# Attention in a two-layer hybrid trunk: probabilities times values in 512-column products, scores of two key groups in alternate banks

## The chip, the cores and the metric

One core of one Trainium2 chip runs the whole program as a single launch. The metric is the device time of that launch in microseconds (us), lower is better; three runs of the kernel before are shown.

## The reference, cut to what matters

The program is two layers of a trunk over 256 tokens of 1024 channels. Each layer has a token mixer (a gated delta-rule branch and a sliding-window attention branch, fed by one input projection, merged by sigmoid gates) and then a channel mixer: dense SwiGLU in layer 0, eight experts in layer 1. The change touches only the attention branch:

```python
# 8 query heads of 64 channels in 2 key groups of 4; chunks of 64 tokens, a window of 2 chunks
s = einsum('bnqhgd,bnkhd->bhgnqk', qc, kb) * (dh ** -0.5)      # scores
m = maximum(max(s, axis=-1), sink)
p = exp(s - m)
denom = sum(p, axis=-1) + exp(sink - m)
p = p / denom
o = einsum('bhgnqk,bnkhd->bnqhgd', p, vb)                      # probabilities times values
```

## The kernel before, in words

Everything runs in float32 or in splits of it. Each weight matrix is streamed in units of 128x2048 through a ring of six buffers; ScalarE (ACT) rounds a unit to its high part `w_hi` (L759 in the mixers, L1046 in the experts), VectorE (DVE) subtracts to get the low part `w_lo` (L1799, L1963), and TensorE (PE) makes three products per tile from the parts (L1130 to L1132, L1124 to L1126). Every engine has its own program written out by hand, in order, and the engines meet through semaphores that only rise; there is no planner. A DMA refill of a ring buffer is issued by the SP queue once DVE has released the unit six places earlier.

The 256 tokens are two blocks `tb` of 128. The attention of one layer is a string of numbered tasks, and `ATT_BANK` says which of the eight PSUM banks each task writes. `scores(tb)` (L1328) makes the scores: block 0 has 128 keys, so four heads fill a bank of 512 columns and there are two banks (0 and 1); block 1 has 192 keys, two heads to a bank, four banks (2, 4, 5, 6). Each bank begins with one bf16 product that writes the mask (L1337, 128 rows of the array), then one float32 product per head (L1343) over the 64 channels of that head. The heads of key group 0 lie in rows 0 to 63 of `a_qT` and `a_kT`, those of group 1 in rows 64 to 127. Before, a bank holds heads of one group only, and the banks are made one after the other: for block 0 bank by bank group 0, then group 1; for block 1 two banks of group 0, then two of group 1. `am0` and `am1` are the masks, `G` = 2 groups, `J` = 4 heads in a group.

DVE takes the row maxima of each bank (L2040 in `row_max`), ACT takes the exponentials head by head (L918 in `exp_scores`), DVE divides (L2055), PE transposes (L1358, L1360 in `turn_p`), ACT copies the transposed probabilities to `a_pt` (L927), and `p_v(tb)` multiplies by the values `a_v`. In `p_v(0)` each head is one product of 128 columns over 128 keys (L1375). In `p_v(1)` each head takes two, one over the 64 keys in rows 64 to 127 (L1372) and one over 128 keys (L1373), which add up in the same 128 columns. All heads of a group use the same `a_v` as stationary operand. ACT and DVE then take the high and low part of the output (L934, L2062).

The order of the work on PE around it, per layer:

```python
                scores(0)
                scores(1)
                two_blocks(("qkvz", l, 7), 3)
                turn_p(0)
                pe.wait_ge(qkn_s, 2 * l + 1)
                pe.wait_ge(pe_s, TB * (l + 1))
                k_products(kT, 6)
                p_v(0)
                turn_p(1)
                pe.wait_ge(att_a, NATT_A * l + 6)
                one_block(("gate", l, 0), 0, 0)
                p_v(1)
```

after which come transposes (L1408), `k_products(qT, 4)` (L1386), the other half of gate 0 and the inversion of the delta rule in levels (from L1417). `warm` and `spread` (L1378) are products with 512 columns; `ada_piece` (L1143) makes products with a single column (L1145).

Of the kernel before, what the change touches and what calls it, by code (L numbers as in the profile page):

```python
# [16 lines left out]
P = 128  # L17
EPS = 1e-6
NEG = -1e30
CHUNK = 64  # L20
# [3 lines left out]
def build_program(nc, x, c, positions, ada_w, ada_b, norm_mix_w, norm_ffn_w, w_in, conv_w, a_log,  # L24
# [4 lines left out]
    T = x.shape[1]  # L29
# [4 lines left out]
    KEYS1 = 3 * CHUNK  # L34
    H = a_log.shape[1]
    DK = P
    NQH = sinks.shape[1]
    DH = CHUNK
    G = 2
    J = NQH // G  # L40
# [79 lines left out]
    for s, k in enumerate(split_keys):  # L120
        if k[0] in ("fg", "fu", "fd"):
# [3 lines left out]
            b, n_ffn = (2 - n_ffn) % NS_FFN, n_ffn + 1  # L125
        elif k == ("qkvz", 1, 0):
            b = 2
        elif k == ("mix", L - 1, 1, 1):
            b, last_in[2] = 2, split_keys.index(("wa", L - 1, 1))
        else:  # L130
            b = s % NS_MIX
# [45 lines left out]
    with ctx:  # L177
# [6 lines left out]
        ps = [ctx.enter_context(nc.psum_tensor(f"bank{b}", [P, 512], F32)) for b in range(8)]  # L184
# [21 lines left out]
        ident_b = sb("ident_b", [P, P], BF16)  # L206
# [55 lines left out]
        a_pt = wk(6144, 16, P)  # L262
        a_qk = wk(8192, TB, 10, DH)
        a_v = wk(10752, TB, P)
        a_qT = wk(9728, J, T)
        a_kT = wk(9472, T)
# [143 lines left out]
        att_ps = sem("attention_in_psum")  # L410
# [93 lines left out]
        ATT_BANK = (0, 1, 4, 0, 1, 2, 4, 5, 6, 0, 1, 4, 5, 0, 1, 2, 3, 2, 3)  # L504
        T_SCORE, T_TURN, T_PV = (3, 5), (9, 13), (11, 17)
# [237 lines left out]
        def _(act):  # L743
# [93 lines left out]
            for l in range(L):  # L837
# [74 lines left out]
                def exp_scores(tb):  # L912
                    keys, per = (P, KEYS1)[tb], (4, 2)[tb]
                    act.wait_ge(mx_s, TB * l + tb + 1)
                    act.activation(smax[:, tb, 3, :], smax[:, tb, 3, :], ACT.Exp)
                    for h in range(NQH):
                        n, m = divmod(h, per)
                        ins = act.activation(a_s[tb][:, h, :], ps[ATT_BANK[T_SCORE[tb] + n]][:, m * keys:(m + 1) * keys],  # L918
                                             ACT.Exp, bias=smax[:, tb, 0, h:h + 1], scale=float(DH) ** -0.5,
                                             accum_out=smax[:, tb, 2, h:h + 1])  # L920
                    ins.then_inc(pe_s, 1)
# [16 lines left out]
                for n in range(2):  # L938
                    b = att(n)
                    act.copy(a_qT[:, 2 * n:2 * n + 2, :].rearrange("p a b -> p (a b)"), b[:]).then_inc(att_a, 1)  # L940
                b = att(2)
# [112 lines left out]
            for n in range(4):  # L1054
                half, tb = divmod(n, TB)
# [65 lines left out]
        def _(pe):  # L1121
# [41 lines left out]
            def tokens(tb):  # L1163
                return slice(tb * P, (tb + 1) * P)
# [82 lines left out]
            for l in range(L):  # L1247
# [17 lines left out]
                else:  # L1265
                    pe.wait_ge(fold_s, 1)
                    for ko in range(KO):
                        ins = pe.matmul(ps[3][:, 0:E], ones[:], w_rs[:, ko, :], start=ko == 0, stop=ko == KO - 1)
# [19 lines left out]
                for kh in range(2):  # L1288
                    wh, wl = parts(("swq", l, kh), 4)
                    for tb in range(TB):  # L1290
                        for kk in range(4):
                            ko = 4 * kh + kk
                            ins = by_token(ps[2 + tb][:], hT_hi[:, ko, tokens(tb)], hT_lo[:, ko, tokens(tb)],
                                           wh[:, kk, :], wl[:, kk, :], ko == 0, ko == KO - 1)
# [6 lines left out]
                for tb in range(TB):  # L1301
                    for ko in range(KO):
                        ins = by_token(ps[tb][:, 0:2 * P + 2 * H], hT_hi[:, ko, tokens(tb)], hT_lo[:, ko, tokens(tb)],
                                       wh[:, ko, :], wl[:, ko, :], ko == 0, ko == KO - 1)
# [8 lines left out]
                for t in (0, 1):  # L1313
                    b = ps[ATT_BANK[t]]
                    for jj in range(2):
                        for tb in range(TB):
                            j = 2 * t + jj
                            ins = pe.transpose(b[:, jj * T + tb * P:jj * T + (tb + 1) * P],
                                               a_qk[:, tb, 2 * j:2 * j + 2, :].rearrange("p g d -> p (g d)"), ident[:])
                    ins.then_inc(att_ps, 1)  # L1320
                pe.wait_ge(ln_s, 4 * (l + 1))
                b = ps[ATT_BANK[2]]
                for tb in range(TB):
                    ins = pe.transpose(b[:, tb * P:(tb + 1) * P],
                                       a_qk[:, tb, NQH:NQH + G, :].rearrange("p g d -> p (g d)"), ident[:])
                ins.then_inc(att_ps, 1)

                def scores(tb):  # L1328
                    keys, per = (P, KEYS1)[tb], (4, 2)[tb]
                    am = (am0, am1)[tb]  # L1330
                    for n in range(NQH // per):
                        b = ps[ATT_BANK[T_SCORE[tb] + n]]
                        if tb and n == 0:
                            pe.wait_ge(qkv_s, 8 * l + 7)
                        if tb and n == 3:
                            pe.wait_ge(exps_s, 6 * l + 2)
                        pe.matmul(b[:, 0:per * keys], ident_b[:], am[:].unsqueeze(1).to_broadcast([P, per, keys]),  # L1337
                                  start=True, stop=False)
                        for m in range(per):
                            h = n * per + m  # L1340
                            g, j = divmod(h, J)
                            rows = slice(g * DH, (g + 1) * DH)
                            ins = pe.matmul(b[:, m * keys:(m + 1) * keys], a_qT[rows, j, tokens(tb)],  # L1343
                                            a_kT[rows, (T - KEYS1 if tb else 0):(T if tb else P)],
                                            start=False, stop=m == per - 1)
                        ins.then_inc(att_ps, 1)

                def turn_p(tb):
                    pe.wait_ge(pn_s, TB * l + tb + 1)
# [14 lines left out]
                def p_v(tb):  # L1364
                    pe.wait_ge(att_a, NATT_A * l + 5 + 4 * tb)
                    for g in range(G):
                        b = ps[ATT_BANK[T_PV[tb] + g]]
                        for j in range(J):
                            h = g * J + j
                            o = b[:, j * P:(j + 1) * P]  # L1370
                            if tb:
                                pe.matmul(o, a_v[CHUNK:P, 0, :], a_pt[CHUNK:P, h, :], start=True, stop=False)  # L1372
                                ins = pe.matmul(o, a_v[:, 1, :], a_pt[:, NQH + h, :], start=False, stop=True)  # L1373
                            else:
                                ins = pe.matmul(o, a_v[:, 0, :], a_pt[:, h, :], start=True, stop=True)  # L1375
                        ins.then_inc(att_ps, 1)

                def spread(lhsT, rows, banks):  # L1378
# [39 lines left out]
                for lev in range(1, LEVELS):  # L1418
                    for tb in range(TB):
                        if lev > 1:  # L1420
                            pe.wait_ge(xx_s, 12 * l + 2 * (lev - 2) + tb + 1)
                        for h in range(H):
                            n = tb * H + h
# [30 lines left out]
                    for tb in range(TB):  # L1454
# [3 lines left out]
                        for h in range(H):  # L1458
                            n = tb * H + h
# [307 lines left out]
        def _(dve):  # L1767
# [204 lines left out]
            for l in range(L):  # L1972
# [60 lines left out]
                def row_max(tb):  # L2033

                    keys, per = (P, KEYS1)[tb], (4, 2)[tb]
                    sm = smax[:, tb]
                    for n in range(NQH // per):
                        t = T_SCORE[tb] + n
                        dve.wait_ge(att_ps, NTASK * l + t + 1)
                        ins = dve.tensor_reduce(sm[:, 0, n * per:(n + 1) * per],  # L2040
                                                ps[ATT_BANK[t]][:, 0:per * keys].rearrange("p (h k) -> p h k", h=per),
                                                AX.X, ALU.max)
                    link(ins)
                    link(dve.scalar_tensor_tensor(sm[:, 1, :], sm[:, 0, :], float(DH) ** -0.5, sink_rows[:, l, :],
                                                  ALU.mult, ALU.max))
                    dve.tensor_tensor(sm[:, 3, :], sink_rows[:, l, :], sm[:, 1, :], ALU.subtract)
                    dve.tensor_scalar(sm[:, 0, :], sm[:, 1, :], -1.0, None, ALU.mult).then_inc(mx_s, 1)
# [438 lines left out]
```

## Time and profile before

| | |
|---|---|
| median of 3 runs | 1776.28 us (1775.56 to 1776.55) |
| span of the profiled execution, first to last instruction | 1772.6 us |
| device time of the profiled execution itself | not listed; against the median the span is 3.7 us shorter |
| TensorE busy | 98% |
| TensorE weight loads busy (beside the products) | 85% |
| VectorE busy | 83% |
| ScalarE busy | 61% |
| bytes read from HBM | 510.90 MB |

How to read it. A busy TensorE is one whose product records follow each other without a hole; a record's length includes the pipeline behind it, so the cost of one product is the distance between starts, not the length. A float32 product appears as two records with a weight load each; a product of the split parts (three per tile) as one. In the profile's chain of waits the work that ended last is followed back, each step to what released it. "Idle before" names the time an engine stood still in front of an instruction, and what ended it.

### The profile page before, as it was taken

To read this page: it belongs to the slowest core of one execution; us is meant where nothing else is said; L and a number is where in the kernel's file an instruction comes from. 1 tells how busy PE (TensorE), PEld (TensorE's weight loads), DVE (VectorE), ACT (ScalarE), POOL (GpSimd) and SP (SyncE) were. 2 spreads that over 40 slices of the span, in tenths; PEclk is the share of its full clock that TensorE was granted. 3 is DMA by queue.
4 is the path that set the end of the run, shared out by engine and by line. 5 is a ranking of instruction groups with operands and counts; after the bars stand their busy time and mean duration, and the time that the engine had idled before them with its cause. 6 is when DMAs were issued, how large, how long until landed. Compare 5 with 4: busy or idle time off the path is not lost.

```text
span 1772.6 us, 26724 instructions
## 1 busy us (share of the span) xinstructions
PE 1734.2 (98%) x10287; PEld 1510.4 (85%) x10290; DVE 1463.5 (83%) x1420; ACT 1085.5 (61%) x953; POOL 73.4 (4%) x131
## 2 busy tenths in 40 slices
PE   7999999999999999999999999999999999999997
PEld 6889999999998889987788888888888888888875
DVE  6978688878768665679988898988889889989898
ACT  4564355333345643567677777777777777777775
POOL 4010000000000100000000000010000000000000
PEclk9999999999999999999999999999999999999999
DMA  9735566988964332469999999999999999999994
GB/s 311 257 125 190 145 236 220 334 303 304 328 224 129 110 95 96 143 241 361 336 369 385 361 372 370 361 390 362 365 386 356 375 381 356 382 370 365 388 392 160
DMA packets 261447, 519.97 MB, mean 293 GB/s; under 512 B 12170, under 2 KB 75892, under 8 KB 261364
## 3 DMA queue, kind: packets, MB, share of 16 engines
q1 hardware_dynamic: 257988, 506.21, 80.4%
q0 software_dynamic: 3376, 12.58, 1.8%
q8 instruction: 60, 0.98, 0.2%
q14 instruction: 23, 0.19, 0.0%
HBM read 510.90 MB, written 7.86 MB: 293 GB/s over the span
## 4 chain that ended last, share of the span: by engine, by line
PE 87%; DVE 8%; ACT 2%; issue 2%; DMA 1%; POOL 0%; DVEq 0%; SPq 0%; ACTq 0%; POOLq 0%
PE bank L1124 17%; PE bank L1126 17%; PE bank L1125 17%; PE bank L1130 9%; PE bank L1131 8%; PE bank L1132 8%; DVE w_lo L1963 2%; DVE w_lo L1799 2%; PE bank L1726 1%; PE bank L1424 1%; PE bank L1461 1%; PE bank L1145 1%; DVE ada_acc L1817 1%; ACT w_hi L1046 1%; DMA ring<-in_ada_w_dram 1%
## 5 line engine op out<-in xcount | busy, mean ns | idle before, releaser
L1963 DVE TENSOR_TENSOR w_lo<-ring,w_hi 128x2048 fp32r<-128x2048 f32 x336 | 766.8, 2289 | 94.8 <-ACT w_hi L1046 90.1
L1046 ACT CAST w_hi<-ring 128x2048 fp32r<-128x2048 f32 x336 | 642.1, 1911 | 137.0 <-PE bank L1126 131.5
L1124 PE MATMUL bank<-w_hi,xg_hi 128*128 128x512 f32 x896 | 357.3, 399 | 0.7 <-DVE w_lo L1963 0.7
L1126 PE MATMUL bank<-w_hi,xg_lo 128*128 128x512 f32 x896 | 353.4, 394 | 0.0
L1125 PE MATMUL bank<-w_lo,xg_hi 128*128 128x512 f32 x896 | 352.9, 394 | 0.0
L1130 PE MATMUL bank<-hT_hi,w_hi 128*128 128x256 f32 x1040 | 300.6, 289 | 5.1 <-DVE w_lo L1799 4.3
L1131 PE MATMUL bank<-hT_lo,w_hi 128*128 128x256 f32 x1040 | 293.7, 282 | 0.0
L1132 PE MATMUL bank<-hT_hi,w_lo 128*128 128x256 f32 x1040 | 293.5, 282 | 0.0
L1799 DVE TENSOR_TENSOR w_lo<-ring,w_hi 128x2048 fp32r<-128x2048 f32 x94 | 214.5, 2289 | 63.3 <-ACT w_hi L759 63.1
L759 ACT CAST w_hi<-ring 128x2048 fp32r<-128x2048 f32 x94 | 179.0, 1907 | 58.3 <-PE bank L1132 57.8
L1130 PEld LDWEIGHTS bank<-hT_hi,w_hi 128*128 128x128 f32 x1040 | 198.4, 191 | 9.2 <-DVE w_lo L1799 4.0
L1124 PEld LDWEIGHTS bank<-w_hi,xg_hi 128*128 128x128 f32 x896 | 168.4, 188 | 42.1 <-issue 2.9
L1126 PEld LDWEIGHTS bank<-w_hi,xg_lo 128*128 128x128 f32 x896 | 168.3, 188 | 40.1
L1125 PEld LDWEIGHTS bank<-w_lo,xg_hi 128*128 128x128 f32 x896 | 168.5, 188 | 37.7
L1131 PEld LDWEIGHTS bank<-hT_lo,w_hi 128*128 128x128 f32 x1040 | 198.5, 191 | 1.9 <-issue 1.9
L1132 PEld LDWEIGHTS bank<-hT_hi,w_lo 128*128 128x128 f32 x1040 | 198.4, 191 | 0.0
L1124 PE MATMUL bank<-w_hi,h_hi 128*128 128x512 f32 x448 | 180.2, 402 | 0.0
L1125 PE MATMUL bank<-w_lo,h_hi 128*128 128x512 f32 x448 | 176.1, 393 | 0.0
L1126 PE MATMUL bank<-w_hi,h_lo 128*128 128x512 f32 x448 | 175.7, 392 | 0.0
L1817 DVE SCALAR_TENSOR_TENSOR ada_acc<-ring,c_silu,ada_acc 128x512 f32<-128x512 f32 x162 | 121.6, 751 | 6.0 <-DMA ring<-in_ada_w_dram 0.6
L1126 PEld LDWEIGHTS bank<-w_hi,h_lo 128*128 128x128 f32 x448 | 84.1, 188 | 19.3
L1124 PEld LDWEIGHTS bank<-w_hi,h_hi 128*128 128x128 f32 x448 | 84.2, 188 | 17.7 <-DVE w_lo L1963 0.2
(434 smaller groups left out, 2011.6 us busy)
## 6 DMA issues: line engine op xcount, KB each, us to landing
ring<-in_moe_w_gate_dram SPq DMA_DIRECT2D x112, 1024.0 KB, 7.4
ring<-in_moe_w_up_dram SPq DMA_DIRECT2D x112, 1024.0 KB, 7.3
ring<-in_moe_w_down_dram SPq DMA_DIRECT2D x112, 1024.0 KB, 7.2
ring<-in_ada_w_dram SPq DMA_DIRECT2D x48, 1024.0 KB, 6.4
ring<-in_w_in_dram SPq DMA_DIRECT2D x38, 1024.0 KB, 5.9
ring<-in_ffn_w_gate_dram SPq DMA_DIRECT2D x14, 1024.0 KB, 7.0
ring<-in_ffn_w_up_dram SPq DMA_DIRECT2D x14, 1024.0 KB, 6.8
ring<-in_ffn_w_down_dram SPq DMA_DIRECT2D x14, 1024.0 KB, 7.0
```

The costliest lines, as they stand in the source:

```text
L759: act.copy(w_hi[buf][:], ring[:, ring_slot, :]).then_inc(hi_ready, 1)
L1046: act.copy(w_hi[MOE_BUF[p % NS_MOE]][:], ring[:, p % RING, :]).then_inc(hi_ready, 1)
L1124: pe.matmul(o, xh, wh, start=start, stop=False)
L1125: pe.matmul(o, xh, wl, start=False, stop=False)
L1126: return pe.matmul(o, xl, wh, start=False, stop=stop)
L1130: pe.matmul(o, wh, xh, start=start, stop=False, skip_group_check=shared)
L1131: pe.matmul(o, wh, xl, start=False, stop=False, skip_group_check=shared)
L1132: return pe.matmul(o, wl, xh, start=False, stop=stop, skip_group_check=shared)
L1145: ins = pe.matmul(ps[bank][:, 4 * q + c:4 * q + c + 1], ada_acc[:, (NQ * l + q) % 2, c * P:(c + 1) * P], ones[:, 0:1], start=not begun, st ...
L1799: dve.tensor_tensor(w_lo[buf_of[s]][:], ring[:, u % RING, :], f32(w_hi[buf_of[s]][:]), ALU.subtract).then_inc(taken, 1)
L1817: ins = dve.scalar_tensor_tensor(acc, w[:, kk, :], ck, acc, ALU.mult, ALU.add)
L1963: dve.tensor_tensor(w_lo[b][:], ring[:, p % RING, :], f32(w_hi[b][:]), ALU.subtract).then_inc(taken, 1)
```

## The change

It does two things. `p_v` now makes one product of 512 columns for the four heads of a key group where it made four of 128 (in block 1 one over the 64 keys, one over the 128, per group). `scores` opens two banks at a time, one for each key group, writes both masks, and then issues the heads in turn: one of group 0 into the first bank, one of group 1 into the second, and so on. In block 1 the banks of a pair now hold heads (0, 1) and (4, 5), then (2, 3) and (6, 7), so `row_max` and `exp_scores` find the heads by a new formula, and the wait for `exps_s` stands before the third bank (task 7) where it stood before the fourth.

```diff
                     for h in range(NQH):
-                        n, m = divmod(h, per)
+                        g, j = divmod(h, J)
+                        n, m = G * (j // per) + g, j % per
...
-                    for n in range(NQH // per):
-                        b = ps[ATT_BANK[T_SCORE[tb] + n]]
-                        if tb and n == 0:
+                    for pair in range(NQH // per // G):
+                        banks = [ps[ATT_BANK[T_SCORE[tb] + G * pair + g]] for g in range(G)]
+                        if tb and pair == 0:
                             pe.wait_ge(qkv_s, 8 * l + 7)
-                        if tb and n == 3:
+                        if tb and pair == 1:
                             pe.wait_ge(exps_s, 6 * l + 2)
-                        pe.matmul(b[:, 0:per * keys], ident_b[:], am[:].unsqueeze(1).to_broadcast([P, per, keys]),
-                                  start=True, stop=False)
+                        for b in banks:
+                            pe.matmul(b[:, 0:per * keys], ident_b[:], am[:].unsqueeze(1).to_broadcast([P, per, keys]),
+                                      start=True, stop=False)
                         for m in range(per):
-                            h = n * per + m
-                            g, j = divmod(h, J)
-                            rows = slice(g * DH, (g + 1) * DH)
-                            ins = pe.matmul(b[:, m * keys:(m + 1) * keys], a_qT[rows, j, tokens(tb)],
-                                            a_kT[rows, (T - KEYS1 if tb else 0):(T if tb else P)],
-                                            start=False, stop=m == per - 1)
-                        ins.then_inc(att_ps, 1)
+                            for g, b in enumerate(banks):
+                                j = pair * per + m
+                                rows = slice(g * DH, (g + 1) * DH)
+                                ins = pe.matmul(b[:, m * keys:(m + 1) * keys], a_qT[rows, j, tokens(tb)],
+                                                a_kT[rows, (T - KEYS1 if tb else 0):(T if tb else P)],
+                                                start=False, stop=m == per - 1)
+                                if m == per - 1:
+                                    ins.then_inc(att_ps, 1)
...
                         b = ps[ATT_BANK[T_PV[tb] + g]]
-                        for j in range(J):
-                            h = g * J + j
-                            o = b[:, j * P:(j + 1) * P]
-                            if tb:
-                                pe.matmul(o, a_v[CHUNK:P, 0, :], a_pt[CHUNK:P, h, :], start=True, stop=False)
-                                ins = pe.matmul(o, a_v[:, 1, :], a_pt[:, NQH + h, :], start=False, stop=True)
-                            else:
-                                ins = pe.matmul(o, a_v[:, 0, :], a_pt[:, h, :], start=True, stop=True)
+
+                        def four(rows, at):
+                            return a_pt[rows, at + g * J:at + (g + 1) * J, :].rearrange("p a b -> p (a b)")
+
+                        if tb:
+                            pe.matmul(b[:], a_v[CHUNK:P, 0, :], four(slice(CHUNK, P), 0), start=True, stop=False)
+                            ins = pe.matmul(b[:], a_v[:, 1, :], four(slice(0, P), NQH), start=False, stop=True)
+                        else:
+                            ins = pe.matmul(b[:], a_v[:, 0, :], four(slice(0, P), 0), start=True, stop=True)
                         ins.then_inc(att_ps, 1)
...
-                        ins = dve.tensor_reduce(sm[:, 0, n * per:(n + 1) * per],
+                        at = J * (n % G) + per * (n // G)
+                        ins = dve.tensor_reduce(sm[:, 0, at:at + per],
```

## Rows read from the trace of the kernel before

**Rows 1.** The page: the span, and TensorE's busy time.
```profile
span 1772.6 us, 26724 instructions
...
PE 1734.2 (98%) x10287; PEld 1510.4 (85%) x10290; DVE 1463.5 (83%) x1420; ACT 1085.5 (61%) x953; POOL 73.4 (4%) x131
```

**Rows 2.** The page: the chain that ended last, by engine.
```profile
PE 87%; DVE 8%; ACT 2%; issue 2%; DMA 1%; POOL 0%; DVEq 0%; SPq 0%; ACTq 0%; POOLq 0%
```

**Rows 3.** Windows: stretch, then busy us and instructions by engine, clock, DMA share, GB/s.
```profile
104.00:111.26 7.26, 7.26 (x40) 4.89 (x38) 4.41 (x9) 5.88 (x20) 0.00 (x0) 1.00 0.03 8
601.79:609.05 7.26, 7.26 (x40) 4.89 (x38) 4.41 (x9) 5.88 (x20) 0.00 (x0) 1.00 0.03 8
...
126.68:133.25 6.57, 6.57 (x33) 4.76 (x33) 3.60 (x4) 0.58 (x1) 0.00 (x0) 1.00 0.21 75
624.47:631.05 6.58, 6.58 (x34) 4.76 (x34) 3.60 (x4) 0.58 (x1) 0.00 (x0) 1.00 0.20 72
...
800.00:1760.00 960.00, 953.89 (x4265) 771.98 (x4264) 863.07 (x648) 693.88 (x460) 38.38 (x31) 1.00 1.00 365
```

**Rows 4.** Timeline of PE through the scores, layer 0: start us, us, instruction.
```profile
104.00 0.38 PE L1337 MATMUL bank<-am,ident_b 128*128 128x512 bf16 x1
104.31 1.16 PE L1343 MATMUL bank<-work 64*128 64x128 f32 x8
105.40 0.39 PE L1337 MATMUL bank<-am,ident_b 128*128 128x512 bf16 x1
...
106.81 0.34 PE L1337 MATMUL bank<-am,ident_b 128*128 128x384 bf16 x1
107.07 0.92 PE L1343 MATMUL bank<-work 64*128 64x192 f32 x4
107.92 0.34 PE L1337 MATMUL bank<-am,ident_b 128*128 128x384 bf16 x1
```

**Rows 5.** Chain of waits, layer 0: what one record costs on PE, by kind.
```profile
104.17 0.22 PE bank L1337
...
134.29 1.79 PE bank L1386 x16
...
138.95 0.79 PE bank L1145 x8
...
141.63 3.44 PE bank L1380 x8
```

**Rows 6.** Timeline of PE in p_v(1), layer 0, to the transposes behind it.
```profile
126.68 0.48 PE L1372 MATMUL bank<-work 64*128 64x128 f32 x2
127.10 0.49 PE L1373 MATMUL bank<-work 128*128 128x128 f32 x2
127.52 0.48 PE L1372 MATMUL bank<-work 64*128 64x128 f32 x2
...
133.25 1.04 PE L1408 MATMUL bank<-ident,work 128*128 128x128 f32 x8
```

**Rows 7.** Timeline of PE: the first product of gate 0, layer 0.
```profile
123.64 0.36 PE L1130 MATMUL bank<-hT_hi,w_hi 128*128 128x256 f32 x1 [0.18 <-DVE w_lo L1799]
```

**Rows 8.** Timeline of DVE from the row maxima to gate 0's low part, layer 0.
```profile
109.13 1.68 DVE L2040 TENSOR_REDUCE smax<-bank 128x2 f32<-128x384 f32 x3
111.37 0.56 DVE L2040 TENSOR_REDUCE smax<-bank 128x2 f32<-128x384 f32 x1 [0.56 <-PE bank L1343]
...
118.22 1.22 DVE L2087 TENSOR_TENSOR work<-work,incl_blk 128x1024 f32<-128x1024 f32 x1
121.20 2.29 DVE L1799 TENSOR_TENSOR w_lo<-ring,w_hi 128x2048 fp32r<-128x2048 f32 x1 [1.76 <-ACT w_hi L759]
```

**Rows 9.** Timeline of ACT: exponentials that `exps_s` counts, and copies behind `turn_p(0)`, layer 0.
```profile
104.21 1.08 ACT L909 ACTIVATE work<-bank 128x512 f32<-128x512 f32 x2 [0.87 <-PE bank L1380]
...
117.75 1.07 ACT L927 COPY work<-bank 128x512 f32<-128x512 f32 x2 [1.87 <-PE bank L1360]
```

**Rows 10.** Who waited for whom: total us, times, longest us.
```profile
ACT ob_hi L934 <- PE bank L1373: 16.9, 4, 5.7
```

## Prediction

> **What bounds the kernel now.** I read the page first: TensorE is busy 98% of a span of 1772.6 us [rows 1], and the chain that ended last lies on it for 87% [rows 2]. Even the long expert stage, where the transfers are in flight all the time, has PE busy for 953.89 of 960 us [rows 3]. So what counts is time on PE, if nothing else becomes late. Next I cut windows around the parts that change. The scores take 7.26 us in either layer, `p_v(1)` takes 6.57 and 6.58 us, PE without a hole in all four, granted clock 1.00 (the level of 2.4 GHz), and hardly any transfer [rows 3]. The two layers are alike to 0.01 us, so I cost layer 0 and double it. Last come the timelines, for the distances between starts, and the chain of waits, for who is late behind.
>
> **The price list of one record.** A float32 product is two records. With 128 columns sixteen of them take 1.79 us: 0.112 each. With 512 columns eight take 3.44 us: 0.43 each. With a single column eight take 0.79 us: 0.099 each; streaming is nothing there, so this is the floor of a weight load and its issue [rows 5]. Four records of 128 columns (0.448) against one of 512 (0.43) is thus almost no gain: merging columns alone pays nearly nothing.
>
> **p_v(1): where the gain of the first part is.** From a 64-row product to the 128-row one behind it is 0.42 us, and 0.42 again to the next 64-row one [rows 6], although two records of 128 columns need 0.224. Each change between a 64-row and a 128-row product therefore costs 0.19 us. The 16 products with 15 changes among them and one of 0.10 at the end make 16 x 0.224 + 15 x 0.19 + 0.10 = 6.5, the window's 6.57. After, there are 4 products of two records with 512 columns, 3 changes, and the exit: 4 x 0.86 + 3 x 0.19 + 0.10 = 4.11. **Saved 2.46 us a layer**; if a change of rows were dearer behind a 512-column product by as much again, 1.9. All of it stands on PE, directly on the chain.
>
> **p_v(0).** Eight products become two: 16 x 0.112 = 1.79 to 4 x 0.43 = 1.72, so 0.07. I cost it at nothing, because gate 0 behind it waits for its low part anyway: PE stands 0.18 us in front of it [rows 7]. That weight chain starts at the transposes of `turn_p(0)` and runs through ACT and DVE, not through `p_v`. Without this cover it would be 0.14 us for both layers.
>
> **Scores, step by step.** A bank of block 0 is 1.40 us start to start, one of block 1 is 1.11 [rows 4]. A mask of 512 columns streams in 0.22 [rows 5], but the first 64-row product starts 0.31 to 0.32 behind it: 0.10 to get in. Eight records of 128 columns are 0.896, and the next mask comes 1.09 after them: 0.19 to get out. In block 1 the mask is 0.16 and 0.10, the four records of 192 columns take 0.85, of which 0.19 is the way out, so 0.165 each. With pairs of banks half of the ways in and out vanish. If the records just follow each other as now, block 0 is 2 x 0.22 + 0.10 + 16 x 0.112 + 0.19 = 2.52 and block 1 is 2 x (0.32 + 0.10 + 8 x 0.165 + 0.19) = 3.86: 6.38 against 7.26, **0.88 saved**.
>
> The unknown is what two products in different rows of the array, one after the other, do. No row shows it: before, no product of rows 0 to 63 stands next to one of rows 64 to 127. The upper bound is that they run side by side. With A, A', B, B' in order, A' streams while B does, and so on: nine record times in place of sixteen, five in place of eight. Block 0 is then 0.44 + 0.10 + 9 x 0.112 + 0.19 = 1.74, block 1 is 2 x (0.42 + 5 x 0.165 + 0.19) = 2.87, together 4.61: 2.65 saved. But every record still has its own load, and the nearest row says that a record doesn't get below 0.099. With that floor block 0 is 0.54 + 16 x 0.099 + 0.19 = 2.31 and block 1 is 2 x (0.42 + 8 x 0.099 + 0.19) + 2 x 0.07 for the last stream = 2.94, together 5.25: **2.0 saved**. I take this one: the streams overlap, the loads don't. The bad end is that each alternation costs like a change of rows, or more; there are 7 in block 0 and 2 x 3 in block 1, 13 a layer (below).
>
> The Trainium skill ("TensorE: Matmul & The Clock Gate", Part 3) says that tiles in different row groups load and multiply concurrently, a few nanoseconds apart. By that rule alone the scores would give the full 2.65, and the time would be 1766.1. The same page (Part 2, LDWEIGHTS) says that a load goes by its columns, whatever its rows, at 1.2 GHz: 107 ns for 128 columns; if loads queue up, the scores would give 1.9 and the estimate would be 1767.6. The single-column row (99 ns) is near the second; neither speaks about float32 halves, and no row here shows two groups at once.
>
> **What could be late next.** Behind the scores PE goes on with `qkvz` 7 (5.8 us), then `turn_p(0)`, at whose end the chain passes to ACT (L927, L899, L759) and DVE (L1799) before gate 0. For PE's 2.0 us to reach gate 0, both must be free 2.0 earlier. ACT stood 1.87 us before L927 [rows 9] and DVE 1.76 before L1799 [rows 8]. They needn't give 2.0 from that: they move too. The four reductions of block 1 (0.56 each) began at 109.13 and the last ran at 111.37, after a wait of 0.56 for its bank [rows 8]. With all banks there by about 109.3 they run through from 109.1 and end 0.6 earlier, so exponentials, both divisions and L2087 come 0.6 earlier, and the holes must give 1.4: ACT 0.47 left, DVE 0.36. With the full 2.65 the holes give some 1.5: still enough. Block 0's maxima lose the head start of their first bank, since both banks end together; that is 0.25 us late at worst (no overlap), where the holes are hardly used. The wait for `exps_s` before task 7: ACT ends those exponentials at 105.3 [rows 9], PE comes there after 107. Queued behind that wait on PE are the last two banks and `qkvz` 7, and DVE's maxima wait for them; with 1.7 us in hand nothing of it shows. The weights of gate 0 have long landed (DMA share 0.03 [rows 3]).
>
> Behind `p_v(1)`, ACT and DVE wait for PE, not PE for them: ACT stood up to 5.7 us for the outputs [rows 10]. `out_high` and `out_low` of group 1 keep their distance to the end of `p_v(1)`, so the delta rule's start keeps its own. No instruction or transfer is added on ACT, DVE, SP or POOL; the refills move with DVE's releases, six units deep. Past this the stages are tied to one another and not to a clock, so the shift carries to the end.
>
> **Sum.** 2.46 + 2.0 = 4.46 a layer, 8.9 in all: the span 1772.6 becomes 1763.7. The 3.7 us between span and median are kept: 1776.3 - 8.9 = **1767.4**.
>
> **The rivals.** A change of over 0.2% is 3.6 us here, about what can be told from nothing.
> 1. Full overlap, loads too: 2.46 + 2.65 = 5.11 a layer, **1766.1**. For it: no row shows that the 0.099 is a port and not the array's own. Against: the floor row.
> 2. The order brings no overlap (the second part doesn't do what it is for): 2.46 + 0.88 = 3.34, **1769.6**. For it: nothing in the trace shows two products at once. Against: `p_v(1)` shows a penalty for a change of mode only, and nothing shows that one is due inside it.
> 3. Each alternation costs one change, 0.19: 13 x 0.19 = 2.47, 0.87 a layer left, **1774.5**. For it: the only row with two row shapes in turn shows exactly that. Against: there the shape changes (64 to 128 rows), here only the place.
> 4. Slower: each alternation costs a full way out and in, 0.38, plus an unhidden load, 0.10: 13 x 0.48 = 6.2, minus 3.34 is 2.9 lost a layer, **1782.1**. It decides for slower from 3.34 / 13 = 0.26 us an alternation. Against: that is above what any single change costs in rows 4 or 6.
> 5. The holes of ACT or DVE are used up, and half of the scores' gain is lost at gate 0: 2.46 + 1.0, **1769.4**; it falls in with the second.
>
> **How the numbers follow.** The forecast (floor of the loads) 0.38, full overlap 0.22, no overlap or half lost 0.28, one change each 0.08, slower 0.04. The range from 1765.2 (full overlap, with 0.9 for its errors) to 1771.8 (no overlap with `p_v(1)` at 1.9, which is 1770.7, and 1.1 over) holds the first three, 0.88, less their tails. Faster takes these: 0.86; within 0.2% has the 0.08 and some of the tails: 0.10; slower 0.04.
>
> **What would show it.** Right: windows of 5.2 us for the scores and 4.1 for `p_v(1)` in either layer, L1343 records of block 1 starting some 0.1 apart, L1372 as two records of 512 columns, and the gate's idle time in front still about 0.2. No overlap would show as 6.4 us of scores with starts 0.112 and 0.165 apart; a penalty as starts 0.3 or more apart where the groups alternate. If gate 0 waits 1 us and more, the holes were too small. The prediction is wrong if `p_v(1)` stays over 5 us, or if the sum of the four windows falls but the span doesn't follow.

## The result, and the profile after

The changed kernel takes 1765.49 us (median of 4 runs, 1764.14 to 1765.89) against 1776.41 us for the kernel before (4 runs, 1775.56 to 1777.51). The ratio is 0.9936, 95% interval 0.9924 to 0.9948: 11.4 us faster, between 9.2 and 13.5. The forecast was 8.9 us: the direction and the two places of the gain hold, and one term, the scores, is too small. The median stands 0.3 us above the lower end of the range (1765.2); the ratio times the median the forecast started from, 1776.28, gives 1764.9, 0.3 us below it. The range was too high at its lower end.

The page of the kernel after: the span, TensorE's busy time, and the chain by engine.

```profile
span 1763.4 us, 26580 instructions
...
PE 1723.6 (98%) x10215; PEld 1497.1 (85%) x10218; DVE 1463.4 (83%) x1420; ACT 1086.1 (62%) x953; POOL 71.8 (4%) x131
...
PE 87%; DVE 8%; ACT 2%; issue 2%; DMA 1%; POOL 0%; DVEq 0%; SPq 0%; ACTq 0%; POOLq 0%
```

Against [rows 1, 2] PE has lost 10.6 us of busy time and 72 product records. DVE has lost nothing, and the chain's shares are the same. The profiled execution took 1765.37 us by its device time, 2.0 us more than its span. The 3.7 us that the forecast kept between span and median of the kernel before are thus more than one execution shows: its profile came from a quicker execution than the three shown. Only the difference was forecast, so this did no harm.

The same four windows as [rows 3], in the kernel after: stretch, then busy us and instructions by engine, clock, DMA share, GB/s.

```profile
105.21:109.39 4.18, 4.18 (x39) 2.55 (x38) 2.40 (x6) 3.54 (x7) 0.00 (x0) 1.00 0.05 17
...
124.83:128.95 4.12, 4.12 (x9) 1.32 (x9) 3.59 (x4) 0.58 (x1) 0.00 (x0) 1.00 0.33 115
597.54:601.72 4.18, 4.18 (x39) 2.55 (x37) 2.39 (x6) 3.54 (x7) 0.00 (x0) 1.00 0.07 20
617.15:621.27 4.12, 4.12 (x9) 1.32 (x9) 3.60 (x4) 0.58 (x1) 0.00 (x0) 1.00 0.37 125
```

The scores take 4.18 us where they took 7.26, so 3.08 saved a layer; `p_v(1)` takes 4.12 where it took 6.57 and 6.58, so 2.45 and 2.46. Twice 3.08 and 2.45 is 11.06 us. Between the two layers nothing moved: from the transposes behind `p_v(1)` of layer 0 to the first mask of layer 1 are 468.54 us before (133.25 to 601.79) and 468.59 after (128.95 to 597.54).

The timeline of PE, layer 0, of the kernel after, to be held against [rows 4, 6, 7].

```profile
105.21 0.59 PE L1339 MATMUL bank<-am,ident_b 128*128 128x512 bf16 x2
105.73 1.16 PE L1345 MATMUL bank<-work 64*128 64x128 f32 x16
106.83 0.50 PE L1339 MATMUL bank<-am,ident_b 128*128 128x384 bf16 x2
107.26 0.92 PE L1345 MATMUL bank<-work 64*128 64x192 f32 x8
108.11 0.50 PE L1339 MATMUL bank<-am,ident_b 128*128 128x384 bf16 x2
108.54 0.92 PE L1345 MATMUL bank<-work 64*128 64x192 f32 x8
...
121.79 0.36 PE L1131 MATMUL bank<-hT_hi,w_hi 128*128 128x256 f32 x1 [0.26 <-DVE w_lo L1803]
124.83 1.12 PE L1376 MATMUL bank<-work 64*128 64x512 f32 x2
125.88 1.13 PE L1377 MATMUL bank<-work 128*128 128x512 f32 x2
126.94 1.12 PE L1376 MATMUL bank<-work 64*128 64x512 f32 x2
127.99 1.12 PE L1377 MATMUL bank<-work 128*128 128x512 f32 x2
128.95 1.04 PE L1412 MATMUL bank<-ident,work 128*128 128x128 f32 x8
```

Read the second line against its like in [rows 4]. Sixteen score records now take from 105.73 to 106.83, 1.10 us with the way out, where eight took 1.09. Eight records of 192 columns take 0.85, as four did. The second group costs next to nothing. `p_v(1)` shows two records of 512 columns per product and 1.05 from one product to the next: 0.86 + 0.19.

Behind the scores, the two engines whose holes had to give way, ACT first, then DVE, in the kernel after (against [rows 8, 9]).

```profile
115.88 1.07 ACT L928 COPY work<-bank 128x512 f32<-128x512 f32 x2 [0.23 <-PE bank L1363]
```

```profile
106.93 1.29 DVE L2045 TENSOR_REDUCE smax<-bank 128x4 f32<-128x512 f32 x2 [2.39 <-PE bank L1345]
...
109.75 1.95 DVE L2045 TENSOR_REDUCE smax<-bank 128x2 f32<-128x384 f32 x4
...
117.99 1.22 DVE L2092 TENSOR_TENSOR work<-work,incl_blk 128x1024 f32<-128x1024 f32 x1
119.35 2.29 DVE L1803 TENSOR_TENSOR w_lo<-ring,w_hi 128x2048 fp32r<-128x2048 f32 x1
```

ACT's hole in front of the copies has gone from 1.87 us to 0.23, DVE's in front of gate 0's low part from 1.76 to none that is listed (0.14 from the end of L2092 to the start of L1803). The four reductions now run without a stop. Where ACT begins the exponentials of block 1, before and after:

```profile
112.44 0.21 ACT L915 ACTIVATE smax<-smax 128x8 f32<-128x8 f32 x1 [1.32 <-DVE smax L2047]
...
112.21 0.21 ACT L915 ACTIVATE smax<-smax 128x8 f32<-128x8 f32 x1 [0.47 <-DVE smax L2052]
```

Counted from the first mask that is 8.44 and 7.00 us, so this work moved 1.44 us earlier and the holes gave the rest. The cover held: gate 0 starts 16.58 us after the first mask (121.79 - 105.21) where it started 19.64 after it (123.64 - 104.00), 3.06 of the 3.08 earlier. Hardly any of it is left.

### The profile page after: what moved, and what is told of

The parts are those of the page before. It is cut to its first block, busy times and chain, and to the rows that moved or that the text cites. A ratio compares the mean times of both kernels' runs of the same rounds, so it can differ in the third digit from the quotient of the medians.

```text
span 1763.4 us, 26580 instructions
## 1 busy us (share of the span) xinstructions
PE 1723.6 (98%) x10215; PEld 1497.1 (85%) x10218; DVE 1463.4 (83%) x1420; ACT 1086.1 (62%) x953; POOL 71.8 (4%) x131
## 4 chain that ended last, share of the span: by engine, by line
PE 87%; DVE 8%; ACT 2%; issue 2%; DMA 1%; POOL 0%; DVEq 0%; SPq 0%; ACTq 0%; POOLq 0%
PE bank L1125 17%; PE bank L1127 17%; PE bank L1126 17%; PE bank L1131 9%; PE bank L1132 8%; PE bank L1133 8%; DVE w_lo L1967 2%; DVE w_lo L1803 2%; PE bank L1730 1%; PE bank L1428 1%; PE bank L1465 1%; PE bank L1146 1%; DVE ada_acc L1821 1%; ACT w_hi L1047 1%; DMA ring<-in_ada_w_dram 1%
## 5 line engine op out<-in xcount | busy, mean ns | idle before, releaser
L1803 DVE TENSOR_TENSOR w_lo<-ring,w_hi 128x2048 fp32r<-128x2048 f32 x94 | 214.6, 2290 | 60.1 <-ACT w_hi L759 59.6
```

Of the source, the lines that this page charges most:

```text
L1803: dve.tensor_tensor(w_lo[buf_of[s]][:], ring[:, u % RING, :], f32(w_hi[buf_of[s]][:]), ALU.subtract).then_inc(taken, 1)
```

## The experiments

Times of kernels run once come with a profile and are read by their windows, not by their totals. Starts are counted from the first mask of the scores, because the run-up to it differs between the profiles by a microsecond and more (see the kernel before once more).

**One half alone: the products with the values.** `p_v` as after, everything else as before.

```diff
-                        for j in range(J):
-                            h = g * J + j
...
+                        if tb:
+                            pe.matmul(b[:], a_v[CHUNK:P, 0, :], four(slice(CHUNK, P), 0), start=True, stop=False)
+                            ins = pe.matmul(b[:], a_v[:, 1, :], four(slice(0, P), NQH), start=False, stop=True)
```

> The products of probabilities and values as after, the scores as before. Both theories of the scores agree here: if the two halves of the change add up, p_v(1) is 4.1 us a layer and the scores stay 7.26 us, so the time is 2 x 2.45 = 4.9 us below before (about 1771.5). If the gain of p_v needs the scores' new order, or is eaten by a wait at the delta rule behind it, less than 3 us.

Measured: 1770.99 us, ratio 0.9967 (0.9954 to 0.9979), so 5.9 us faster, between 3.7 and 8.2. Its PE timeline:

```profile
104.97 0.38 PE L1337 MATMUL bank<-am,ident_b 128*128 128x512 bf16 x1
...
124.61 0.36 PE L1130 MATMUL bank<-hT_hi,w_hi 128*128 128x256 f32 x1 [0.25 <-DVE w_lo L1800]
127.65 1.12 PE L1373 MATMUL bank<-work 64*128 64x512 f32 x2
...
131.77 1.04 PE L1409 MATMUL bank<-ident,work 128*128 128x128 f32 x8
```

`p_v(1)` takes 4.12 us. Gate 0 starts 19.64 us after the mask, exactly as before, although `p_v(0)` is 0.07 shorter: its gain went into the idle time in front of the gate, 0.25 where it was 0.18 [rows 7].

**The other half alone: the scores.** `scores`, `row_max` and `exp_scores` as after, `p_v` as before.

```diff
-                    for n in range(NQH // per):
+                    for pair in range(NQH // per // G):
...
+                            for g, b in enumerate(banks):
```

> The scores as after, the products of probabilities and values as before. If overlap of the two groups explains what the forecast missed, the scores are 4.18 us a layer in place of 7.26, gate 0 starts 3.0 us earlier, and the time is 6.1 us below before (about 1770.3). If ACT's and DVE's holes are too small, gate 0 comes less than 2.6 us earlier and the time falls by under 5.2 us.

Measured: 1769.52 us, ratio 0.9956 (0.9939 to 0.9972), so 7.8 us faster, between 5.0 and 10.8. The scores start at 104.95 and gate 0 at 121.52, 16.57 us apart as in the kernel after. The halves add up in the windows (3.08 and 2.45 us a layer); the totals, 5.9 and 7.8 us, are higher than twice these, and agree with them within their intervals.

**Is it the order? Groups in blocks within a pair of banks.** Masks, banks and changes of rows as after.

```diff
-                        for m in range(per):
-                            for g, b in enumerate(banks):
+                        for g, b in enumerate(banks):
+                            for m in range(per):
```

> As after, but within a pair of banks all heads of group 0 go first, then all of group 1: the same banks, masks and changes of rows, another order. If the products overlap only with the neighbour in program order, one overlap is left in each pair: scores 2.28 + 2 x 1.61 = 5.5 us. If nothing overlaps across blocks, 6.4 us. If TensorE reaches far ahead for the other rows, 4.2 us as after, and the order issued in turn was not needed.

Measured, PE timeline:

```profile
105.04 0.59 PE L1339 MATMUL bank<-am,ident_b 128*128 128x512 bf16 x2
105.56 1.71 PE L1345 MATMUL bank<-work 64*128 64x128 f32 x16
107.20 0.50 PE L1339 MATMUL bank<-am,ident_b 128*128 128x384 bf16 x2
107.63 0.93 PE L1345 MATMUL bank<-work 64*128 64x192 f32 x8
108.49 0.50 PE L1339 MATMUL bank<-am,ident_b 128*128 128x384 bf16 x2
```

None of the three: the scores take 4.74 us (105.04 to 109.78). In block 1 (two heads, then two) the overlap is whole, eight records in 0.86 us. In block 0 (four heads, then four) the sixteen take 1.64 us, less 0.19 for the way out 1.45: thirteen record times of 0.112, three hidden in place of eight. So TensorE begins the other rows' products while several of the first are still queued, but only so far ahead. The score instructions alone, in the first 0.56 us of block 0, in the kernel after, then in this one (stretch, then busy us and number of products and of weight loads, clock, DMA share, GB/s):

```profile
105.72:106.28 0.56, 0.55 (x8) 0.55 (x10) 1.00 0.14 29
...
105.55:106.11 0.56, 0.55 (x4) 0.55 (x5) 1.00 0.16 29
```

Here group 0 is alone in that stretch.

**How far ahead: two heads of each group in turn.**

```diff
-                        for m in range(per):
-                            for g, b in enumerate(banks):
+                        for m0 in range(0, per, 2):
+                            for g, m in ((0, m0), (0, m0 + 1), (1, m0), (1, m0 + 1)):
+                                b = banks[g]
```

> As after, but two heads of group 0, then two of group 1 (block 1 then has the order of the kernel with pairs in blocks, where eight records took 0.85 us with the way out). If TensorE reaches at least four records ahead for the other rows, block 0's sixteen records take 1.09 us with the way out, as after. If it reached only to its neighbour, 1.09 + 0.22 = 1.3 us. If the reach is counted in time and not in records, block 0 could lie between.

Measured, PE timeline:

```profile
105.62 1.26 PE L1346 MATMUL bank<-work 64*128 64x128 f32 x16
106.82 0.50 PE L1339 MATMUL bank<-am,ident_b 128*128 128x384 bf16 x2
```

1.20 us against 1.10 in turn: one record time lost, between the first two cases. The starts of single records in the traces of this kernel and the one in blocks show the reach, and it is counted in records:

- In blocks, four heads and four: the fifth product of group 0 starts at 106.111, and the first weight load of group 1 at 106.115. Three products of group 0 still wait then. In layer 1 it is 599.057 and 599.061.
- In blocks, two heads and two: group 0's first load starts at 107.631 and group 1's at 107.645, with three products of group 0 waiting.
- Two heads in turn, second half of block 0: the fifth product of group 0 starts at 106.174, the fifth load of group 1 at 106.178, again with three waiting (598.594 and 598.598 in layer 1). That load would have been due one record time earlier, which is the one that is lost.

So three waiting products of the other rows are passed here, and a fourth isn't. Issue time doesn't explain it: in block 1 group 1's load, the fifth in order, starts 0.014 us behind the first, and in block 0 the ninth comes 0.554 behind it. What holds the fourth isn't shown. In turn is the order that needs the least of it.

**Is it the rows or the banks? In turn into alternate banks, but both from rows 0 to 63.** Group 1's heads get group 0's scores here, so part of the computation is another.

```diff
-                                rows = slice(g * DH, (g + 1) * DH)
+                                rows = slice(0, DH)
```

> As after, in turn into alternate banks, but both groups read rows 0 to 63 (group 1 gets the scores of group 0's heads; that is left wrong). If it is the different rows that let two products run at once, nothing overlaps and the scores take 2.5 + 2 x 1.94 = 6.4 us. If alternate banks alone do it, 4.2 us as after.

Measured, PE timeline:

```profile
105.77 2.05 PE L1345 MATMUL bank<-work 64*128 64x128 f32 x16
107.75 0.50 PE L1339 MATMUL bank<-am,ident_b 128*128 128x384 bf16 x2
108.18 1.56 PE L1345 MATMUL bank<-work 64*128 64x192 f32 x8
109.67 0.50 PE L1339 MATMUL bank<-am,ident_b 128*128 128x384 bf16 x2
```

1.98 us for sixteen and 1.49 for eight: one after the other (16 x 0.112 + 0.19, 8 x 0.165 + 0.19). This is what the prediction wrote for no overlap: 6.35 us in all, 6.38 there. The different rows make the overlap; alternate banks alone don't. Whether the second bank is needed as well isn't shown: alternating rows into one bank would have two products write one bank at once, and it wasn't tried.

**What pays in p_v(1): fewer changes, or wider products?** Products of 128 columns as before, four with 64 rows first, then four with 128.

```diff
+                        for j in range(J if tb else 0):
+                            h = g * J + j
+                            pe.matmul(b[:, j * P:(j + 1) * P], a_v[CHUNK:P, 0, :], a_pt[CHUNK:P, h, :], start=j == 0,
+                                      stop=False, skip_group_check=True)
                        for j in range(J):
...
-                                pe.matmul(o, a_v[CHUNK:P, 0, :], a_pt[CHUNK:P, h, :], start=True, stop=False)
```

> Scores as after; p_v with products of 128 columns as before, but in p_v(1) the four 64-row products of a group go first and its four 128-row ones follow. If the gain of p_v(1) comes from fewer changes of rows, it takes 16 x 0.224 + 3 x 0.19 + 0.10 = 4.25 us a layer, nearly what the merged products take (4.12). If merging the columns is what pays, it stays near 6.5 us.

Measured, PE timeline:

```profile
124.93 1.16 PE L1373 MATMUL bank<-work 64*128 64x128 f32 x8
126.02 1.16 PE L1379 MATMUL bank<-work 128*128 128x128 f32 x8
127.10 1.16 PE L1373 MATMUL bank<-work 64*128 64x128 f32 x8
...
129.18 1.04 PE L1415 MATMUL bank<-ident,work 128*128 128x128 f32 x8
```

4.25 us. Of the 2.45 us, 2.32 come from the order alone and 0.13 from the 512 columns on top of it.

**Two more changes taken away: both 64-row products first.**

```diff
+                    if tb:
+                        older(0)
+                        older(1)
...
-                            pe.matmul(b[:], a_v[CHUNK:P, 0, :], four(slice(CHUNK, P), 0), start=True, stop=False)
```

Here `older(g)` is the removed product, for group `g`.

> As after, but in p_v(1) the 64-row products of both groups go first, then both 128-row ones: two changes of rows fewer. If a change costs 0.19 us, p_v(1) takes 4.12 - 0.38 = 3.74 us a layer. If the cost is paid per product and not per change, 4.1 us. The output of group 0 comes later by 0.7 us, which ACT and DVE should cover.

Measured: from 123.58 to 127.32, 3.74 us, as the 0.19 per change has it; the stages behind keep their distance to its end (6.33 us to the delta rule's start in layer 0, as in the kernel after). The total, 1765.44 us, doesn't show the saving; what hides it is in the next paragraph.

**The kernel before once more.** The same kernel, profiled a second time, shows what differs without any edit.

> The kernel before, profiled once more. If the 1.2 us by which the changed kernels reach their scores later is the start of a single execution and not the change, this profile reaches its first mask at 105 us and not at 104.00, and its span is near 1774.5.

Measured: first mask at 104.08, span 1774.3, device time 1776.07 us. The first half of the expectation fails, the second holds: this profile repeats the early start. Of the twelve profiles three have it, the two of the kernel before and the kernel with both 64-row products first (103.98); the other nine, the kernel after among them, reach the scores at 104.93 to 105.48. The two kinds differ in TensorE's granted clock on the way: from 26.9 to 40.6 us it is 0.88 in the three (before: full but for some 3.4 us at the level of 1.2 GHz) and 0.51 to 0.64 in the nine (after: the level of 1.2 GHz nearly throughout). Just ahead of it, from 20.0 to 26.9 us, TensorE is busy without a hole in the kernel before as in the kernel after. All of this lies ahead of anything the change touches, and one kernel with the whole change has the early start, so the change doesn't bring the 1.2 us with it by necessity; what sets the clock there isn't shown. From the transposes behind `p_v(1)` of layer 1 to the end are 1141.6 us in the first profile of before, 1143.0 in this one (631.26 to 1774.3) and 1142.1 in the kernel after. This stretch goes with the clock as well. In three profiles (the first of before and the last two kernels below) it never falls there, and the stretch is 1141.6 to 1142.0 us; in eight TensorE runs some 3.4 us at the lower level between 759 and 780 us, and it is 1142.1 to 1143.4; and in the kernel with groups in blocks 6.8 us, and it is 1145.1. TensorE was busy without a hole in the 15 us ahead of it in the kernel after (745.0 to 760.6). Of the 1765.44 us of the kernel with both 64-row products first, 1143.4 are this stretch. So single spans differ by 1.5 us and more on work that the change doesn't touch; the windows at full clock repeat within 0.02. The 9.2 us between the first two spans are the 11.06, less 1.21 for the run-up, 0.58 for the end and 0.05 between the layers.

**A version beyond the change.** Both 64-row products first, the masks of block 1's four banks ahead of all its products, and on DVE gate 0's low part ahead of the mask of `X`; then the same without the edit on DVE.

```diff
-                        if tb and pair == 1:
-                            pe.wait_ge(exps_s, 6 * l + 2)
-                        for b in banks:
...
+                        for n in range(NQH // per if pair == 0 else 0):
+                            if tb and n == 3:
+                                pe.wait_ge(exps_s, 6 * l + 2)
...
-                link(dve.tensor_tensor(X, X, wide(incl_blk[:], [P, TB * H, P], 1), ALU.mult))
                 ahead(("gate", l, 0), 0)
+                link(dve.tensor_tensor(X, X, wide(incl_blk[:], [P, TB * H, P], 1), ALU.mult))
```

> After, with three edits: the 64-row products of both groups first in p_v(1) (as measured, 0.38 us a layer), the four masks of block 1 ahead of all its products (one way in and out less, 0.29 us), and on DVE the low part of gate 0 ahead of the mask of X. The scores should take 4.18 - 0.29 = 3.89 us. ACT had only 0.23 us in hand before the copies of turn_p(0), so gate 0 should start 16.36 us after the first mask (16.58 in the kernel after). Sum 0.6 us a layer, 1.2 in all: about 1764.3, ratio to before about 0.993. If the later first pair of block 1 delays DVE's maxima, gate 0 stays at 16.6.

> The same without the edit on DVE. If DVE's hole before gate 0's low part is used up in the kernel after (0.1 us left), gate 0 starts 16.45 us or more after the first mask and not 16.36, although the scores take 3.89 us here too. If DVE still has room, both kernels show 16.36.

Measured with the edit on DVE: 1763.23 us, ratio 0.9923 (0.9909 to 0.9936) to before. Its interval overlaps that of the change, so the totals don't part the two; the windows do. PE timeline:

```profile
104.93 0.59 PE L1339 MATMUL bank<-am,ident_b 128*128 128x512 bf16 x2
...
106.55 0.82 PE L1339 MATMUL bank<-am,ident_b 128*128 128x384 bf16 x4
107.30 1.57 PE L1345 MATMUL bank<-work 64*128 64x192 f32 x16
108.80 0.39 PE L1131 MATMUL bank<-hT_hi,w_hi 128*128 128x256 f32 x1
...
121.12 0.36 PE L1131 MATMUL bank<-hT_hi,w_hi 128*128 128x256 f32 x1
...
127.89 1.04 PE L1419 MATMUL bank<-ident,work 128*128 128x128 f32 x8
...
625.37 0.82 PE L1435 MATMUL bank<-work 128*128 128x128 f32 x5 [0.23 <-DVE work L2118]
```

The scores take 3.87 us, gate 0 starts 16.19 after the mask (16.36 expected; 16.58 in the kernel after), and `p_v(1)` ends 22.96 after it (23.74). That is 0.78 us a layer. In layer 1 part of it goes again: the moved DVE work makes the delta rule's start 0.38 us later (5.91 us behind the transposes, where it was 5.53; 5.54 without the edit on DVE), with 0.23 of waiting for DVE in the row. ACT has nothing left either: its copies now follow its exponentials with no wait that is listed, and DVE stands 0.89 us for `w_hi`. Without the edit on DVE:

```profile
105.48 0.60 PE L1339 MATMUL bank<-am,ident_b 128*128 128x512 bf16 x2
...
121.95 0.36 PE L1131 MATMUL bank<-hT_hi,w_hi 128*128 128x256 f32 x1 [0.41 <-DVE w_lo L1810]
```

16.47 us and 0.41 of idle time in front of the gate: DVE's cover was indeed used up, and only 0.11 of the 0.31 gets through.

## Why the prediction was right or wrong

**p_v(1), 2.46 us: right**, 2.45 and 2.46 in the two layers, and for its reason. The prices from the trace (0.43 a record of 512 columns, 0.19 a change) gave 4.11 against 4.12, and the sorted kernel confirms that the changes and not the width pay. The worse bound of 1.9 didn't come: a change costs 0.19 behind a wide product too.

**p_v(0) at nothing: right**; its 0.07 shows as more idle time before gate 0, in the kernel with that half alone.

**Scores, "the streams overlap, the loads don't", 2.0 us: this step failed.** It is the term of the sum that was mis-sized: 3.08 measured. With two sets of rows in turn a record costs 0.057 on average (1.10 less 0.19 for the way out, over sixteen), far below the floor of 0.099, so the loads of different rows overlap as well. The Trainium skill ("TensorE: Matmul & The Clock Gate", Part 3) has it so, loads and products of different row groups running together; the trace agrees, with these 0.057.

**The floor was also misread.** The weight loads behind that row, in the kernel before:

```profile
138.67 0.98 PEld L1145 LDWEIGHTS bank<-ones,ada_acc 128*128 128x128 f32 x8
139.57 1.53 PEld L1424 LDWEIGHTS bank<-work 128*128 128x128 f32 x13
```

Eight loads take 0.90 us, 0.112 each, and the single products start 0.112 apart too, but for the first two (0.026). The piece of 0.79 us in [rows 5] runs from the end of the first product to the end of the eighth, which is seven distances and not eight. So within one set of rows a record of one column costs what a record of 128 does. With 0.112 for the floor the prediction's own step would have saved about 1.6 a layer and given 1768.2; that it came as near as 2.0 was luck. Its other estimate, with loads of 107 ns in a queue, leaves out the term for the last stream: it comes to 1.75 and 1767.9, not 1.9 and 1767.6.

**The upper bound was too low as well.** It let the second group start one record behind the first: nine record times of sixteen, five of eight, 2.65 us. The records show eight and four. The two groups set off together, their first products 0.007 us apart. The rest of the miss is that two masks in a row and the way in take 0.52 and 0.43 us, not 0.54 and 0.42, which is nothing. With 3.08 in place of 2.0 the sum is 11.06 and the forecast would have been 1765.2. The range's lower end stood on that wrong bound with 0.9 us taken off, and so had no room left for a run that came out a little lower.

**Rivals.** Full overlap was the right one, at 1766.1 and with 0.22 of the chance, and too small by the record times above, three a layer. No overlap is what the scores do when both groups use the same rows; its sum of 6.38 was measured there as 6.35. A price on each alternation, and with it the slower case, falls: the way through sixteen alternating records is no longer than that through eight. The groups have one shape of rows, and only a change of shape costs.

**What could be late next: right in its outcome, and tighter than said.** The fifth rival, holes used up, didn't come. Forecast were 0.47 and 0.36 us left on ACT and DVE at a shift of 2.0; at 3.06 there are 0.23 and about 0.1. One term behind it was mis-sized and helped: block 1's exponentials, and the divisions behind them, moved up by 1.44 us and not by 0.6. The prediction let the reductions of block 1 begin where they did; they begin 0.59 earlier (4.54 us behind the mask, where it was 5.13), because block 0's second bank is ready sooner too, and running through gives 0.85. With 0.6 alone the holes would have had to give 2.46 us, more than the 1.87 and 1.76 there were. So it was in part luck that nearly the whole 3.08 reached gate 0. That the cover ends there is shown by the last pair of kernels.

## What to carry to other kernels

In this kernel products over half the rows of the array cost the full price (0.112 us a record of 128 columns, with 64 rows as with 128) unless one over the other half is near them: issue the two halves in turn, into different banks, and the second costs next to nothing, in float32 too. Keep products of one row shape together, since each change of shape between float32 products costs 0.19 us here, more than a 128-column record. Widening products that already stream back to back pays hardly anything (0.13 of 2.45 us), and a saving of this size should be checked against the holes of the engines behind it before more is taken.

## What was not expected of the hardware

A single-column float32 product costs as much as one of 128 columns within one set of rows, 0.112 us a record, and neither is a floor for alternating rows: 0.057 in turn. TensorE starts a product past queued ones of the other rows, so products don't always start in the order of the program: three waiting ones are passed, a fourth isn't. In the order two heads and two heads of 192 columns all four records were hidden, in the order four heads and four heads of 128 columns only three of eight, and with two and two in turn one was lost.
